# The second query pair of two attention branches, made ahead of the branch's first z tile

## What is computed

```python
h  = rmsnorm(x, norm_w) * (1 + scale) + shift
p  = h @ w_in                                   # keys, values, queries, z and g of all branches
q_s = rope(sq);  q_a = rope(rmsnorm(aq, ax_q_norm))
o_m = dense_latent_attention(q_m, k_m, v_m, ...)
o_s = window_latent_attention(q_s, k_s, v_s, ..., sink)
o_a = dense_latent_attention(q_a, k_a, v_a, ...)
y_b = (o_b * silu(z_b)) @ w_o_b                 # b in m, s, a
y   = sigmoid(g_m) * y_m + sigmoid(g_s) * y_s + sigmoid(g_a) * y_a
x   = x + gate * (y @ w_out)
```

## Time and profile before

| | us |
|---|---|
| median of 3 runs | 1871.46 (1869.13 to 1875.13) |
| the profiled execution: its time | 1863.98 |
| its span | 1861.9 |
| PE busy | 1732.5 |
| DVE busy | 1088.5 |
| ACT busy | 1047.0 |
| POOL busy | 518.3 |

### The profile page before, as it was taken

The page is one execution under the profiler, slowest core; times in us unless marked ns, Lnnn a source line. Parts: engine busy times, 40 slices in busy tenths (PEclk is TensorE's granted clock), DMA queues, the critical chain, the costliest instruction groups (busy, mean ns, idle before and its releaser), DMA issues.

```text
span 1861.9 us, 26973 instructions
## 1 busy us (share of the span) xinstructions
PE 1732.5 (93%) x10550; PEld 1512.3 (81%) x10550; DVE 1088.5 (58%) x2183; ACT 1047.0 (56%) x1915; POOL 518.3 (28%) x296
## 2 busy tenths in 40 slices
PE   7999989999999899999999999989799988999897
PEld 2777878889998789888889977868778867888777
DVE  6534776665555566555675653666565555556534
ACT  3434777666656677665221433766566657776332
POOL 1522222122222222221322343322133222232342
PEclk9998989999999999999999999989999999999999
DMA  8111011011111112112535231111112221212542
GB/s 313 37 35 27 24 32 35 16 48 43 55 46 35 40 41 52 35 44 80 183 119 181 78 116 34 33 30 35 35 46 59 66 68 36 57 51 57 181 141 91
DMA packets 174301, 127.40 MB, mean 68 GB/s; under 512 B 21533, under 2 KB 163423, under 8 KB 174176
## 3 DMA queue, kind: packets, MB, share of 16 engines
q1 hardware_dynamic: 170018, 113.27, 21.4%
q10 hardware_dynamic: 2878, 8.24, 1.2%
q0 software_dynamic: 1280, 4.20, 0.7%
HBM read 121.49 MB, written 4.19 MB: 68 GB/s over the span
## 4 chain that ended last, share of the span: by engine, by line
PE 74%; DVE 10%; ACT 8%; POOL 3%; issue 3%; DMA 1%; SPq 0%; DVEq 0%; ACTq 0%; POOLq 0%
PE acc L1312 54%; PE wide L1368 6%; PE ptp L1388 6%; PE pv L1401 4%; PE pv L1402 3%; DVE nmax L1941 2%; DVE pt L1966 2%; ACT e L1632 1%; POOL w_lo L1756 1%; DMA w_raw<-in_ada_w 1%; ACT w_hi L1550 1%; POOL h_lo L1794 1%; DVE k_s L1504 1%; ACT pt L1647 1%; ACT e L1639 1%
## 5 line engine op out<-in xcount | busy, mean ns | idle before, releaser
L1756 POOL TENSOR_TENSOR w_lo<-w_raw,w_hi 128x1024 fp32r<-128x1024 f32 (+4 forms) x188 | 382.9, 2040 | 1168.1 <-ACT w_hi L1550 1167.9
L1312 PE MATMUL acc<-h_hi,w_hi 128*128 128x512 f32 (+2 forms) x1320 | 467.7, 355 | 25.3 <-POOL w_lo L1756 8.4
L1312 PE MATMUL acc<-h_hi,w_lo 128*128 128x512 f32 (+2 forms) x1320 | 464.4, 353 | 0.0
L1312 PE MATMUL acc<-h_lo,w_hi 128*128 128x512 f32 (+2 forms) x1320 | 460.5, 352 | 0.4 <-POOL h_lo L1794 0.3
L1647 ACT ACTIVATE pt<-ptp 128x512 fp32r<-128x512 f32 (+3 forms) x312 | 166.0, 562 | 261.9 <-PE ptp L1388 261.2
L1941 DVE TENSOR_REDUCE nmax<-wide 128x1 f32<-128x768 f32 (+3 forms) x240 | 189.8, 791 | 200.8 <-PE wide L1368 199.2
L1312 PEld LDWEIGHTS acc<-h_hi,w_hi 128*128 128x128 f32 (+1 forms) x1320 | 250.4, 190 | 67.3 <-issue 16.0
L1312 PEld LDWEIGHTS acc<-h_hi,w_lo 128*128 128x128 f32 (+1 forms) x1320 | 250.0, 189 | 34.0
L1312 PEld LDWEIGHTS acc<-h_lo,w_hi 128*128 128x128 f32 (+1 forms) x1320 | 248.0, 189 | 35.6 <-POOL h_lo L1794 0.8
L1966 DVE TENSOR_TENSOR pt<-ptp,pt 128x512 fp32r<-128x512 f32 (+3 forms) x312 | 192.0, 640 | 54.1 <-ACT pt L1647 53.8
L1639 ACT ACTIVATE e<-e,einv 128x768 f32<-128x768 f32 (+3 forms) x240 | 193.3, 806 | 51.2 <-DVE einv L1958 50.4
(11 more groups left out here) (210 smaller groups left out, 3130.2 us busy)
## 6 DMA issues: line engine op xcount, KB each, us to landing
w_raw<-in_w_in SPq DMA_DIRECT2D x102, 512.0 KB, 3.9
w_raw<-in_ada_w SPq DMA_DIRECT2D x48, 512.0 KB, 5.1
w_raw<-in_w_out SPq DMA_DIRECT2D x16, 512.0 KB, 3.6
w_raw<-in_w_o_mla SPq DMA_DIRECT2D x16, 256.0 KB, 2.8
w_raw<-in_w_o_swa SPq DMA_DIRECT2D x16, 256.0 KB, 2.8
w_raw<-in_w_o_ax SPq DMA_DIRECT2D x16, 256.0 KB, 2.9
w_raw<-in_mla_w_uq SPq DMA_DIRECT2D x16, 144.0 KB, 2.3
xres<-in_x SPq DMA_DIRECT2D x2, 1024.0 KB, 17.4
```

What stands on the lines that cost most here:

```text
L1312: ins = nc.tensor.matmul(dst, lhs, rhs, start=first, stop=last)
L1756: nc.gpsimd.tensor_tensor(w_lo[s][:, 0:k], w_raw[s][:, 0:k], f(w_hi[s][:, 0:k]), ALU.subtract).then_inc(w_lo_ready, 1)
```

## The change

Two conditions of the queue. In the second branch the second pair (t = 0 in the loop, heads 2 and 3) no longer waits for z tile (1,0) but only for the first pair, and becomes able when the scores of the last head of the first branch are issued. In the third branch the second pair waits for y tile 7 of the first branch instead of z tile (2,0). All later pairs of the second branch lose the condition on z tile (1,0) too, which is finished by then; those of the third keep theirs.

```diff
@@ -776,8 +776,8 @@
             y_item(0, 2 * t)
             if t + 1 < KO:
                 z_item(1, t + 1)
-                item((SWA, t + 1), SWA, tile_cost, lambda s, t=t: t == 0 or (SWA, 2 * t - 1) in s, q_pair(SWA, t + 1),
-                     urgent=True, after=[("z", 1, 0), (SWA, t)])
+                item((SWA, t + 1), SWA, tile_cost, lambda s, t=t: (("mla", HEADS - 1) if t == 0 else (SWA, 2 * t - 1)) in s, q_pair(SWA, t + 1),
+                     urgent=True, after=[(SWA, t)])
                 y_item(0, 2 * t + 1)
         item("table_a", SWA, 0, lambda s: True, lambda: step_of(lambda: load_table("s")), urgent=True, after=[(SWA, KO - 1)])
         item("keys_a", AX, 0, lambda s: (SWA, HEADS - 1) in s, keys_a, urgent=True, after=["table_a"])
@@ -790,7 +790,7 @@
             if t + 1 < KO:
                 z_item(2, t + 1)
                 item((AX, t + 1), AX, tile_cost, lambda s, t=t: t == 0 or (AX, 2 * t - 1) in s, q_pair(AX, t + 1),
-                     urgent=True, after=[("z", 2, 0), (AX, t)])
+                     urgent=True, after=[("y", 0, 2 * KO - 1) if t == 0 else ("z", 2, 0), (AX, t)])
             y_item(1, 2 * t + 1)
```

## The result

Before 1868.38 us (median of 20 runs), after **1875.05** (20 runs): ratio **1.0039**, 95% interval 1.0025 to 1.0053. The change makes the kernel slower by 0.4%, 7 us (6.7 by the medians, 7.3 by the ratio). The forecast was 13 us faster, 1858.4, with a range to 1872. The profiled execution of after has a span of 1871.4 us, before 1861.9.

The account below looks back on a forecast made before the run. PE, busy 93% of the span, was taken to bound the kernel, with waits and low clock at four boundaries to win. Terms 3.4 + 1.9 + 5.1 + 2.7 = 13.1 us take the median 1871.46 to 1858.4; range 1851 to 1872.

Parts of the forecast that it names:

- Comes back 0.9: Layer 0, second branch: PE's wait at the first value product grows by 0.9 us, leaving a net gain of 3.4.
- 1.2: Layer 0, third branch: 1.2 us comes back, 0.9 plus the pair's squares on ACT; net gain 1.9.
- about even: Layer 0, second branch, ACT's queue: weight splits (1.99 us) go ahead of the closing, short eviction and high part (1.27) come in.
- the 1.44 us: Layer 0, second branch: clock loss over 378 to 382 us, won back with no idle stretch left.
- The gain of 2.7: Layer 1, third branch: net gain of 2.7 us from waits covered by the pair's parts and half the clock loss.
- rival D: The pair isn't made at the boundary: PE would wait for late weights instead, time stays at 1871; chance 0.04.
- the 5.1 us: Layer 1, second branch: net gain of 5.1 us, 5.6 of waits gone less 0.5 coming back.
- B, the chain as the pace: Rival: the attention chain sets the pace, waits return one by one in later units; 1871, give or take 5; chance 0.18.
- C: Rival: the pair's conversion gets in front of the closing at each boundary, 5.3 us a boundary; slower, 1879.6; chance 0.08.
- A': Rival: two table switches in layer 1's third branch hold ACT twice as long as shown, 2.6 us more; 1861.0; chance 0.06.
- my own 0.5: Layer 1, third branch: 0.5 us lost to table loads for the square root and next exponential, ahead of the closing.
- rule of the shared port: Layer 0 closing: DVE's hold by POOL moves ahead of the closing, so the return of 0.9 would be nothing.

Follow-up runs that it names:

- e5: Layer 0 alone changed, both branches, with the second pair's high and low parts due 9000 planner nanoseconds after eviction instead of 4500; 1.0003 against before.
- e6: As e5, with the pair's last context part also made one unit earlier, before the closing; 1.0007 against before.
- e7: Layer 0 alone as changed, queues left as they are, with three more z-tile parts (2.85 us) for TensorE in the unit that closes a branch; 1.0008 against before.
- e2: Only layer 0's third branch changed, the other three boundaries as before; 1.0025 against before.
- e9: Layer 0 alone changed, the second pair's nine parts dealt two a unit in the first two units and five in the closing unit; 1.0027 against before.
- e10: All four boundaries changed, with the dealing of e9 in layer 0 and that of e8 in layer 1; 1857.94 us, 0.9949 against before.
- e3: Only layer 1's second branch changed, the other three boundaries as before; 0.9987 against before.
- e8: Layer 1 alone changed, the pair's parts dealt two a unit from the branch's start, none in the unit before it; 1853.38 us, 0.9924 against before.
- e11: Layer 0 alone as changed, with the second pair's high and low parts due 800 planner nanoseconds after eviction instead of 4500; 1.0061 against before.

## Why the prediction was wrong

**What bounds the kernel** was right: PE's waits at the four boundaries, and the clock. That layer 1 holds a gain was right too. Three steps failed.

**"Comes back 0.9" and "1.2" in layer 0**, the terms that decided the sign. They were 4.1 and 4.5: the wait at the first value product grew from 0.34 to 4.43, and from none to 4.51. I had counted one part less of cover on PE's side and called ACT's queue "about even", because two weight splits went ahead as a conversion came in. I never did that sum for DVE, which makes the awaited half of `pt` and makes no high half of weights: nothing left its queue, and 0.86 + 1.39 us came in, 0.98 + 1.39 in the third branch. The whole, from the closing unit's scores (PE L1368, at 377.82 before and 380.88 after) to the start of `pt` on DVE: 10.55 us before, 12.26 after, 1.7 more. In the third branch (632.26 and 635.29) 8.33 and 12.46, 4.1 more: 2.5 behind `og_lo`, 1.6 ahead of it, where DVE now shuffles and rotates the pair (0.74 + 0.69) and an `o_t` beside POOL's rotation takes 1.09 in place of 0.42. On PE's side the work between scores and value product fell from 10.94 to 8.57 us in the second branch, 2.4 less, and from 9.45 to 8.68 in the third, 0.8 less. 1.7 + 2.4 is the 4.1; 4.1 + 0.8, less 0.4 by which `pt` had been early, the 4.5. Of the 2.4, the missing part is 0.95; most of the rest is clock: before, PE did the start of this work at 0.64, now at 1.00, so the 1.44 us that I booked as won on the clock was work that the wait then swallowed; and the lower level came back behind the wait (1.6 us over 394 to 400). e5 and e6 took the two conversions away (1.4, then 1.2 and 0.9 us), e7 bought the cover back. Layer 0's old waits went as forecast, and so did the count of the fill: 7.3 us ahead of the value product before, 6.4 after, by the matmuls that stand there.

**The clock behind it.** In the changed kernel the idle time moved and grew into one piece; in the third branch the lower level cost 5.7 us behind it, where before lost none. That is the greater part of B's 6.5. PE's idle time in B grew by 2.4 us (4.5 to 6.9): 1.4 at the boundary, the new wait of 4.5 less the old ones of 3.1, and 1.0 in mid branch, where waits of 1.00, 0.58 and 0.68 are new (at 715, 745 and 777) and one of 0.52 is gone. With 5.7 of clock and less the 0.9 of work that moved to A, that is 7.2, of 6.5 measured. How much a wait costs in clock isn't settled by its length: the second branch's 4.43 cost 1.6 us, and of the third branch's waits the same 4.51 cost 5.1 in e2 (0.59 over 647.53 to 660), 3.10 cost 1.7 (0.83 over 640 to 650 in e5), and 1.20 + 0.57, in e7, 0.8 + 2.6 in the two windows. That the wait brought the level down is the reading of these rows, no run tells the one apart from the other; and what sets the size stays open. The Trainium skill (TensorE: Matmul & The Clock Gate, Part 1) says that the moment at which the gate changes depends on how the work falls on a free-running count; the rows agree as far as C, where nothing was changed in it, came out between 164.0 and 168.4 us, with granted clocks to match (0.99 at 165.5, 0.97 at 168.4), depending on what was done ahead of it, and as A and B of e9 and e10 differ by 1.0 us on the same work.

**The dealing in layer 1's third branch.** I had one part in unit 207, three in 208, one in 209. But unit 207 counts the pair's own rest as due by the end of the second branch, with one unit left, and spends it whole. That is rival D in another dress (the pair isn't made *there*), which I had tied to late weights only. The gain of 2.7 was measured as 0 (+0.8 of loss on equal work); with the parts in place it was 6.0. The wait for the pair's split, put at 0.6, was 0.42 (1541.50). In the second branch the hand count (4 parts, 2, 0) was right, and the 5.1 us came out at 2.2 (e3) and 3.8 (after). What I missed there is that 1.47 would not "stay" but grow to 2.71, as the two parts spent early were worth more later: dealt out two a unit they gave 6.7.

**Rivals.** B, the chain as the pace, lost: e8 wins 13 us by filling three units at each boundary of layer 1, and of the new waits in mid branch that it asked for there is 1.0 us in the third branch of layer 0. C got the place right, the copies of `pt` behind the pair's conversion, and the decisive size nearly (4.1 to 4.5 us a boundary in layer 0 against its 5.3), but I bound it to four boundaries and to ACT held by POOL; e11 shows that hold, and e7 in mid branch, after doesn't. Its sign, a wait of 3 us or more for `pt` ahead of the new branch's first value product, came true at both boundaries of layer 0. I gave it 0.08 with the lag of 4.5 us of PE time as the argument against. The lag was no protection: it counts PE time, and put the high part exactly behind the split. A', the table loads, isn't it, though an even D is just what its 2.6 us would have made of the 2.7. The two switches that it priced, and my own 0.5 with them, weren't made: with the pair's squares taken ahead of unit 208, its square root ran at 1549.48 on the table loaded at 1538.99, and L1582 has nine loads in place of ten. Nor does a load hold ACT beyond its row: at the one of 1552.13 the instruction ahead ends at 1552.11, the row at 1553.41, and the next starts at 1553.42. The Trainium skill's rule of the shared port (SBUF — State Buffer, Who interferes with whom) had the hold of 2.36 us go ahead of the closing and save the return: the first came true (1.91 us at 380.27, while POOL splits), the second didn't, as the maximum, `o_t` and the split of `og` stand behind it in the queue.

**Open:** why the whole change measured 7.3 us and its stretches 3.9, and what sets how long the lower clock lasts.

## What to carry to other kernels

When work is moved into a gap of the bound engine, redo the sum of each engine's in-order queue at the point where the next hand-over happens, for the engine that makes the awaited tile first of all; a move that leaves an engine's total alone can still put 2 us in front of a copy. Fill is worth most in even small doses: the same five or six parts gave 0 to 4 us when spent at once and 6 to 7 when dealt out two to a unit behind the start of the branch. Where a planner deals by "what is still due over what is left", check by its own list where the moved parts land.

## What I had not expected of the hardware

One wait of 4.51 us in the middle of dense work was followed by 11.4 us in which PE was busy all the time and still had the 1.2 GHz level (granted clock 0.50 over 648.48 to 659.89), 5.7 us lost; one of 4.43 us in the same kernel was followed by 1.6 us lost, and before's waits of 1.16 and 1.98 a few us earlier in the same place by none (1.00). And stretches of 240 to 260 us came back within 0.3 us in four kernels with before's layer 0, though the whole time scatters by 14 in twenty runs (1861.5 to 1875.1): a stretch of the trace told effects of 2 us that twelve timed runs did not. Two kernels with another layer 0, the same in both, differ by 1.0 us, so one profile doesn't tell effects below that.
